# Two transformer blocks on one core: own buffers for the first four weight units, a new order of the element-wise steps in the feed-forwards, and an earlier turning of the second expert block's rows

## What is computed

```python
def reference(x, ...):
    x = first_block(x, ...)      # rms_norm, h @ w_in (5 x 512 + 288 + 2048 columns), fox attention, sparse attention, gates, w_out,
                                 # then x + hierarchical_moe(rms_norm(x)): 16 experts, 2 of them per token, SwiGLU, width 512
    return second_block(x, ...)

def second_block(x, ...):
    f = swiglu(rms_norm_2(h, ffn1_pre_g), ffn1_w_gu, ffn1_w_down)     # D_FF = 2816
    h = h + 0.5 * rms_norm_2(f, ffn1_post_g)
    ...                                                              # neighbourhood and latent attention, w_out
    f = swiglu(rms_norm_2(h, ffn2_pre_g), ffn2_w_gu, ffn2_w_down)
    h = h + 0.5 * rms_norm_2(f, ffn2_post_g)

def swiglu(h, w_gu, w_down):
    gate, up = jnp.split(h @ w_gu, 2, axis=-1)
    return (jax.nn.silu(gate) * up) @ w_down
```

## Time and profile before

| what | us |
|---|---|
| median of 3 runs (lowest, highest) | 1979.58 (1977.93, 1980.55) |
| the profiled execution, its own time | 1979.71 |
| span of the profiled execution | 1977.9 |
| PE busy in it | 1811.5 |
| DVE busy, ACT busy | 966.3, 858.6 |
| mean granted clock of TensorE | 0.947 |

### The profile page before, as it was taken

One profiled execution on the slowest core, in us unless ns is written; L12 is line 12 of the kernel. 1 busy time (PEld: TensorE's weight loads), 2 busy tenths in 40 slices (PEclk: granted clock), 3 DMA queues, 4 the chain that ended last, 5 costly groups with the idle time before them and its releaser, 6 DMA issues.

```text
span 1977.9 us, 22533 instructions
## 1 busy us (share of the span) xinstructions
PE 1811.5 (92%) x8483; PEld 1428.6 (72%) x8483; DVE 966.3 (49%) x1548; ACT 858.6 (43%) x1355; POOL 254.5 (13%) x313
## 2 busy tenths in 40 slices
PE   6997999999859999969999999898788989999997
PEld 5785566666748888857888888786564768888886
DVE  2536444435358999964332342634555353413434
ACT  4234555553237888853222222424566142213222
POOL 3100342320001111110000000331223000000000
PEclk8998899999969999988999999998789989999999
DMA  5323111113568999672323322233000123233331
GB/s 161 107 67 107 43 44 43 44 43 117 202 232 328 383 386 391 264 248 76 107 85 96 106 85 96 87 108 112 12 22 22 46 77 102 85 96 107 87 104 53
DMA packets 161283, 246.31 MB, mean 125 GB/s; under 512 B 11586, under 2 KB 117281, under 8 KB 148256
## 3 DMA queue, kind: packets, MB, share of 16 engines
q1 hardware_dynamic: 152880, 232.30, 34.8%
q0 software_dynamic: 8304, 12.69, 2.1%
HBM read 239.15 MB, written 12.61 MB: 127 GB/s over the span
## 4 chain that ended last, share of the span: by engine, by line
PE 83%; DVE 6%; ACT 4%; issue 3%; DMA 1%; POOL 1%; SPq 0%; DVEq 0%; ACTq 0%; POOLq 0%
PE psum L425 24%; PE psum L426 23%; PE psum L427 23%; PE psum L570 3%; PE psum L590 3%; PE psum L559 2%; ACT warea_r L410 2%; DVE warea_r L416 1%; PE psum L1232 1%; DMA warea<-in_w_in 1%; POOL arena L690 1%; PE psum L1138 1%; PE psum L1020 1%; DVE xarea L2214 1%; PE psum L1401 0%
## 5 line engine op out<-in xcount | busy, mean ns | idle before, releaser
L416 DVE TENSOR_TENSOR warea_r<-warea,warea_r 128x2048 fp32r<-128x2048 f32 x114 | 268.0, 2353 | 388.7 <-ACT warea_r L410 388.5
L425 PE MATMUL psum<-tarea_r,warea_r 128*128 128x512 f32 x896 | 358.2, 400 | 5.9 <-DVE arena_r L2235 3.9
L426 PE MATMUL psum<-tarea_r,warea_r 128*128 128x512 f32 x896 | 351.7, 393 | 0.0
L427 PE MATMUL psum<-tarea_r,warea_r 128*128 128x512 f32 x896 | 351.4, 392 | 0.0
L410 ACT ACTIVATE warea_r<-warea 128x2048 fp32r<-128x2048 f32 x114 | 217.2, 1907 | 303.2 <-PE psum L427 288.4
L425 PE MATMUL psum<-warea_r,arena_r 128*128 128x512 f32 (+1 forms) x768 | 300.8, 392 | 15.1 <-DVE arena_r L2180 7.3
L427 PE MATMUL psum<-warea_r,arena_r 128*128 128x512 f32 (+1 forms) x768 | 297.2, 387 | 0.0
L426 PE MATMUL psum<-warea_r,arena_r 128*128 128x512 f32 (+1 forms) x768 | 297.1, 387 | 0.0
L425 PEld LDWEIGHTS psum<-tarea_r,warea_r 128*128 128x128 f32 x896 | 169.5, 189 | 48.3 <-issue 7.7
L427 PEld LDWEIGHTS psum<-tarea_r,warea_r 128*128 128x128 f32 x896 | 169.9, 190 | 36.3
L426 PEld LDWEIGHTS psum<-tarea_r,warea_r 128*128 128x128 f32 x896 | 169.8, 190 | 34.1 <-issue 0.7
(11 more groups left out here) (321 smaller groups left out, 2436.2 us busy)
## 6 DMA issues: line engine op xcount, KB each, us to landing
warea<-in_ffn_w_gu SPq DMA_DIRECT2D x88, 512.0 KB, 4.9
warea<-in_w_in SPq DMA_DIRECT2D x48, 512.0 KB, 4.7
warea<-in_ffn_w_down SPq DMA_DIRECT2D x40, 512.0 KB, 4.4
arena<-in_w_up SPq DMA_DIRECT2D x16, 1024.0 KB, 7.3
tarea<-in_w_up SPq DMA_DIRECT2D x16, 1024.0 KB, 7.7
tarea<-in_w_down SPq DMA_DIRECT2D x16, 1024.0 KB, 8.0
warea<-in_w_gate SPq DMA_DIRECT2D x14, 1024.0 KB, 7.8
harea<-in_w_gate SPq DMA_DIRECT2D x14, 1024.0 KB, 8.1
```

The source lines that it names most:

```text
L416: dve.tensor_tensor(w_lo[:, u % 2, :], raw[:, u % RAW, :], w_hi[:, u % 2, :].bitcast(f32), ALU.subtract)\
L425: nc.tensor.matmul(out, high, by_high, start=first, stop=False)
L426: nc.tensor.matmul(out, high, by_low, start=False, stop=False)
L427: return nc.tensor.matmul(out, low, by_high, start=False, stop=last)
```

## The change

Five edits.

1. Units 0 to 3 are loaded into buffers of their own in the arena (`EARLY = 4`, `raw_of`, `unit_in`), with a semaphore each. Loads wait for a `split_low` only from unit 6 on. Unit 0 is issued after the second tile of `x`; unit 1 only when the fourth tile has landed, and all behind it. POOL issues the gain column first and holds its other small loads until the fourth tile and unit 0 have landed.
2. In a feed-forward chunk, ACT writes the high half of the hidden chunk ahead of `split_high(v + 2)`, and DVE the low half ahead of `split_low(v + 2)`.
3. `row_factor` of halves 0 and 2 stands right behind PE's chunk 0.
4. In expert round 0 PE turns the rows of block 1 ahead of the last of the four units of `gate_up(0)`; ACT's `slot_high(1)` waits for all of `gate_up(0)` (`moe_done` 8), since the halves have one buffer.
5. Semaphores: `mask_in` becomes `const_in` at 32; three of the bias table's loads on POOL become one and a chained memset; the wait between the two additions of the experts' results (L2214) is on DVE's own step counter in place of `y_used`.

```diff
+EARLY = 4
+    def raw_of(u):
+        return carve(2048 * u, 2048) if u < EARLY else raw[:, u % RAW, :]
+    def unit_in(u):
+        return (s[f"early{u}"], 32) if u < EARLY else (raw_in[u % RAW], 32 * ((u - EARLY) // RAW + 1))
...
-        act.wait_ge(raw_in[u % RAW], 32 * (u // RAW + 1) + (i * 16))
+        sem, value = unit_in(u)
+        act.wait_ge(sem, value + (i * 16))
...
             def feed(u):
-                if u >= RAW:
+                if u >= EARLY + RAW:
                     sp.wait_ge(s["split_lo"], u - RAW + 1)
...
                 sp.dma_start(xres[:, t, :], w["x"][0, t * P:(t + 1) * P, :]).then_inc(s[f"rows_in{t}"], 16)
-            for u in range(2):
-                feed(u)
+                if t == 1:
+                    feed(0)
+            sp.wait_ge(s["rows_in3"], 16)
+            feed(1)
...
             gain_column(0, "norm_mix_g", "col_in0")
+            pool.wait_ge(s["rows_in3"], 16)
+            pool.wait_ge(s["early0"], 32)
...
-            nc.gpsimd.memset(rpbs[0:120, :], 0.0).then_inc(s["rpb_zero"], 1)
-            pool.wait_ge(s["rpb_zero"], 1)
+            chained(nc.gpsimd.memset(rpbs[0:120, :], 0.0))
...
+                    if i == 2 and isinstance(b, int) and b == 0:
+                        slot_features(1)
...
                 gate_up(b)
-                slot_features(b + 1)
                 if not first:
+                    slot_features(b + 1)
                     down(b - 1, 4)
...
                     for k in range(2):
-                        if g % 2 == 0 and isinstance(v, int) and v == 1 and k:
-                            row_factor((2, 4)[g // 2], ps[7])
...
                     mm.then_inc(s["unit_done"], 1)
+                    if g % 2 == 0 and isinstance(v, int) and v == 0:
+                        row_factor((2, 4)[g // 2], ps[7])
...
             def slot_high(b):
+                if isinstance(b, int) and b == 1:
+                    act.wait_ge(s["moe_done"], 8)
...
                     nc.scalar.activation(sgb[:, v % 2, :], sgb[:, v % 2, :], ACT.Silu).then_inc(s["ff_silu"], 1)
-                    split_high(u0 + v + 2, i)
                     act.wait_ge(s["gated"], i + (base + v + 1))
                     at = hid_hi[:, v, :] if isinstance(i, int) else hid_hi[:, ds(i + v, 1), :].rearrange("p a q -> p (a q)")
                     nc.scalar.activation(at, sgb[:, v % 2, :], ACT.Copy).then_inc(s["hid_high"], 1)
+                    split_high(u0 + v + 2, i)
...
-                    split_low(u0 + v + 2, i)
                     dve.wait_ge(s["hid_high"], i + (base + v + 1))
...
                     V.tensor_tensor(lo, sgb[:, v % 2, :], hi.bitcast(f32), ALU.subtract).then_inc(s["ff_hid"], 1)
+                    split_low(u0 + v + 2, i)
...
-            dve.wait_ge(s["mask_in"], 16)
+            dve.wait_ge(s["const_in"], 32)
```

More of the change, by code:

```diff
@@ L340, in build_blocks @@
     Rp = nc.dram_tensor("rpb_padded", (H * 15, 64), f32, kind="Internal").ap()
-    names = """rows_in0 rows_in1 rows_in2 rows_in3 ident_in const_in mask_in col_in0 cols_late moe0 moe1 moe2 moe3 moe4 moe5 moe6 moe7 moe8 moe9 moe10 moe11
+    names = """rows_in0 rows_in1 rows_in2 rows_in3 early0 early1 early2 early3 ident_in const_in col_in0 cols_late moe0 moe1 moe2 moe3 moe4 moe5 moe6 moe7 moe8 moe9 moe10 moe11
         moe_hi moe_lo moe_done gain_in gain_used head_gain_in pos_in misc_in
@@ L402, in unit_through @@
         eng.wait_ge(s[sem], i + value)
+    def raw_of(u):
+        return carve(2048 * u, 2048) if u < EARLY else raw[:, u % RAW, :]
+    def unit_in(u):
+        return (s[f"early{u}"], 32) if u < EARLY else (raw_in[u % RAW], 32 * ((u - EARLY) // RAW + 1))
     def split_high(u, i=0):
         act = nc.scalar
-        act.wait_ge(raw_in[u % RAW], 32 * (u // RAW + 1) + (i * 16))
+        sem, value = unit_in(u)
+        act.wait_ge(sem, value + (i * 16))
         if u >= 2:
             unit_through(act, u - 2, i)
-        act.activation(w_hi[:, u % 2, :], raw[:, u % RAW, :], ACT.Copy).then_inc(s["split_hi"], 1)
+        act.activation(w_hi[:, u % 2, :], raw_of(u), ACT.Copy).then_inc(s["split_hi"], 1)
     def split_low(u, i=0):
@@ L415, in split_low @@
         dve.wait_ge(s["split_hi"], i + (u + 1))
-        dve.tensor_tensor(w_lo[:, u % 2, :], raw[:, u % RAW, :], w_hi[:, u % 2, :].bitcast(f32), ALU.subtract)\
+        dve.tensor_tensor(w_lo[:, u % 2, :], raw_of(u), w_hi[:, u % 2, :].bitcast(f32), ALU.subtract)\
             .then_inc(s["split_lo"], 1)
@@ L740, in feed @@
                     if width == 288 and cols == 8:
-                        dst = raw[:, u % RAW, 0:k * width].rearrange("p (c n) -> p c n", c=k)[:, :, at:at + cols]
+                        dst = raw_of(u)[:, 0:k * width].rearrange("p (c n) -> p c n", c=k)[:, :, at:at + cols]
                     else:
-                        dst = raw[:, u % RAW, at:at + k * width].rearrange("p (c n) -> p c n", c=k)[:, :, 0:cols]
-                    sp.dma_start(dst, src).then_inc(raw_in[u % RAW], 16)
+                        dst = raw_of(u)[:, at:at + k * width].rearrange("p (c n) -> p c n", c=k)[:, :, 0:cols]
+                    sp.dma_start(dst, src).then_inc(unit_in(u)[0], 16)
             masks = NCONST - CONSTS["na_mask"][1]
@@ L762, in _ @@
             sp.wait_ge(s["gate_scaled"], 16)
-            sp.dma_start(const[:, masks:NCONST], w["consts"][:, masks:NCONST]).then_inc(s["mask_in"], 16)
+            sp.dma_start(const[:, masks:NCONST], w["consts"][:, masks:NCONST]).then_inc(s["const_in"], 16)
             def expert_unit(b, i, e):
@@ L991, in _ @@
             pool.wait_ge(s["fd_psum"], 16)
-            nc.gpsimd.memset(rpbs[0:120, :], 0.0).then_inc(s["rpb_zero"], 1)
-            pool.wait_ge(s["rpb_zero"], 1)
[L994 to L997, removed]
+            chained(nc.gpsimd.memset(rpbs[0:120, :], 0.0))
+            pool.dma_start(rpbs[0:120, 16:47], w["na_rpb_2"][0].rearrange("h a b -> (h a) b")).then_inc(s["rpb_moved"], 16)
+            pool.wait_ge(s["rpb_moved"], 16)
+            pool.dma_start(Rp, rpbs[0:120, :]).then_inc(s["rpb_moved"], 16)
+            pool.wait_ge(s["rpb_moved"], 32)
             for h in range(H):
@@ L2211, in _ @@
                 for k in range(2):
[L2212 to L2216, removed]
+                    ins = V.scalar_tensor_tensor(out=xres[:, t, :], in0=Yt[t][:, D * k:D * k + D],
+                                                 scalar=wts[:, 4 * k + t:4 * k + t + 1], in1=xres[:, t, :],
+                                                 op0=ALU.mult, op1=ALU.add)
+                    if k == 0:
+                        chained(ins)
+                ins.then_inc(s["res_ready"], 1)
             raw_low(2)
```

6 lines of the change are left out of this document (3 added, 3 removed).

## The result

| | before | after |
|---|---|---|
| median, us (lowest, highest; runs) | 1978.76 (1975.79, 1980.55; 4) | 1958.47 (1957.22, 1959.91; 4) |
| span of the profiled execution | 1977.9 | 1957.7 |
| mean granted clock | 0.947 | 0.953 |

The ratio is 0.9899, with a 95% interval of 0.9882 to 0.9916: 20.3 us faster, where 16.8 were forecast. A later series of the same kernel gave 1959.78 against 1977.54, a ratio of 0.9908 [0.9895, 0.9921], or 17.8 us. The two intervals overlap. The estimates are 18 and 20 us, and the two intervals together reach from 16 to 23 us, so that more was won than the forecast's 16.8 is not shown.

The account below looks back on a forecast made before the run. PE's work, 83% of the chain that ended last, bounds the kernel, so only its waits and their clock losses can be won. -7.0 - 7.4 - 2.9 + 0.5 = -16.8 from 1979.6 gives 1962.8; range 1957 to 1968.5.

Parts of the forecast that it names:

- The beginning: First loads: x and unit 0 land at 12.6, PE's first product starts at 14.8 instead of 21.82, 7.0 us won.
- Clock at the beginning: PE's first products: still 5.6 us at 0.50 of its clock, so nothing counted, with 0 to 2.8 us to be had.
- Collision of POOL and DVE: After the beginning: POOL's squares start 0.03 us before DVE's split and block it 3.4 us; no gain counted.
- rival (a): Beginning gives more: DVE starts ahead of POOL, or full clock from the first product; 1958 to 1960, chance 0.14.
- Starts of halves 0 and 2: Feed-forward starts: row factor 5.4 us sooner, PE's 1.97 us wait and 1.7 us of clock go, twice; 7.4 us won.
- Ends of the halves: Last feed-forward chunk: PE's wait of 0.74 us for the low half goes in four halves, 2.9 us won.
- Experts: Between expert rounds: ACT now waits for round 0's last product, 0.5 us lost (0.3 to 0.7).
- Attention: Attention stage between the feed-forwards: the prediction gave no term for it.
- (b): First landing bound elsewhere: x and unit 0 complete at 16.8, or unit 1 late; 1967 to 1970, chance 0.16.
- (c): Beginning: POOL's load issues hold DVE's splits of units 0 and 1, at most 14 us; 1977, chance 0.04.
- (d): Steady feed-forward chunks: the later split makes PE wait, up to 1.4 us in each of 44; up to 2023, chance 0.04.

Follow-up runs that it names:

- that run: The changed kernel with DVE's split of unit 2 ahead of three small copies that wait for PE: 1953.77 against 1976.44, ratio 0.9885.

## Why the prediction was right

The time of 1958.47 lies in the range, 4.3 us under the forecast. By its steps:

- **The beginning, -7.0.** Right in mechanism and nearly in size. Forecast and found: last tile of x landed at 12.6 and 12.48, first product 14.8 and 15.18, unit 1's split on ACT no later than 20.5 (18.27 to 20.19). From the last tile's landing to the first product it took 2.7 us and not 2.2: PE had begun on the third tile only at 11.28, sixteen transposes at 0.23 us each kept it until 14.95, and the fourth tile stood behind the third. The landing came from the middle of two bounds, so its closeness is partly luck. The forecast blamed unit 1, the constants and POOL's loads alike; only the runs showed that POOL's loads were the disturbing part (3.5 us), that the held units and constants were no part of it (0.1 us), and that unit 0's place among the x tiles goes with the rest.
- **Clock at the beginning, 0 of 0 to 2.8.** Here the forecast was too low at first and right in the end. The first products ran slow for 1.5 us instead of 5.6, and the kernel was 9.6 us ahead at 48 us; the rest of that rise came behind unit 2's wait. Near 200 us it lost it again, from 10.2 us ahead to 7.4. The windows of the kernel before and of the changed one, over the same work:

```profile
200.00:220.00 20.00, 18.17 (x64) 9.46 (x63) 7.72 (x20) 10.48 (x23) 4.27 (x5) 0.71 0.34 105
```

```profile
190.00:210.00 20.00, 18.45 (x47) 9.33 (x48) 6.85 (x18) 8.31 (x17) 2.14 (x3) 0.56 0.34 106
```

  0.71 - 0.56 over 20 us is 3.0 us of full-clock work less. It does not come with the change each time: the second profiled execution of the changed kernel had 0.69 in its window from 190 to 210 and kept its lead of 9.2 us there, while the run with edit 1 alone lost 2.8. So such gains come and go. Why the clock stays low longer in one execution than in another stays open.
- **Collision of POOL and DVE.** It stayed, as the forecast had it, with 0.03 us between the two; the half of rival (a) that hung on it did not occur.
- **Starts of halves 0 and 2, -7.4.** 7.8 found. The row factor came at 900.42, 7.3 us in front of 907.7 because the kernel was 7.2 ahead, and the low half and the split followed as worked out. The 1.7 us of clock were real: PEclk stayed at 1.00, and the 3.9 us at each start are 2.13 of stall and 1.7 of clock. The run with edit 2 alone shows that the two edits are not a sum there.
- **Ends of the halves, -2.9.** This is the mis-sized term: 4.1 found, in four steps of 1.0 to 1.1 for waits of 0.74. The idle time in a row counts from the modelled end of the last matmul, 0.39 us behind its start, but in a running stream the next one starts 0.23 behind. A wait of 0.74 thus delays the next start by 0.90, and the first interval behind it was 0.33 (1027.59 to 1027.92) instead of 0.23: together 1.0. The same 0.16 is in each long stall: from 919.24 to 921.60 it is 2.36 from start to start, 2.13 more than 0.23, against the 1.97 of the row.
- **Experts, +0.5.** 0.48, by the same path as written: ACT's start moved to the last product.
- **Attention, 0.** 1.0 us came there (13.2 ahead to 14.2), and no edit has a part in it. The difference swings between 12.5 and 15.5 around 1380 us. Over the same work the granted clock was 0.73 in the kernel before (1360 to 1410) and 0.82 in the changed one (1347 to 1397), but 0.77 in the changed kernel's second execution (1346 to 1396), which lost 3.4 us against the first in this stage. The 1.0 us is within what two executions of one kernel differ by.
- **Rivals.** (b), a landing bound elsewhere, fell with 12.48. (c), POOL's issues hold DVE, fell: both splits took 2.29 us at 11.92 and 20.23 while POOL issued from 12.77 on. (d), the steady chunks wait, fell: the waits for a split are three with 7.4 us, as they were before (7.5). But the mechanism of (d) is not idle, since in the run with edit 2 alone it costs 2.67 us where the chunk starts late. (a), more from the beginning, was nearest: the time lies in its range of 1958 to 1960. The extra of its clock was spent by 215 us, and what the trace shows over the forecast, 20.1 against 16.8, is made up of the ends (1.2), the attention (1.0), the starts (0.4) and the beginning with the experts (0.7). Of these only the ends and the starts recur from trace to trace; the rest is of the size of the spread between two executions.

## What to carry to other kernels

When a wait is taken away by a new order in a queue, look at what is now last in that queue, and whether its first round starts late: edit 2 alone turned a wait of 1.97 us into one of 2.67, and with the late start cured it paid in full. Work that is moved earlier into a single buffer gains nothing until the buffer has a twin: 0.48 us lost with one, 2.7 won with two, both against the kernel before. A short stall of TensorE costs more than its row says, here 1.0 us for 0.74.

## What was not expected of the hardware

- **Small loads of another queue cost a large transfer more than large ones of its own.** POOL's loads in flight beside x and unit 0: first product 3.5 us later. A megabyte of unit 1 and the other constants issued right behind x on SP: 0.1 us.
- **The transposes run at the slow rate while the column says 1.00.** In the changed kernel the first thirty-two take 0.23 us each in windows with PEclk 1.00, those of the earlier trace rows 0.13 each, those of the earlier trace rows 0.25 each in a stretch at 0.50. So at the start of this program the column did not show the rate; the duration of a known instruction did. With earlier products on PE the transposes of the last two tiles took 0.14. Products are not needed for it: in the kernel before, where the third tile came 0.59 us after the second was through and not 2.32, the last two tiles took 1.41 and 1.10 us, 0.18 and 0.14 each, with only transposes ahead of them:

```profile
9.68 1.41 PE L1020 MATMUL psum<-const,xarea 128*128 128x128 f32 x8 [0.59 <-DMA xarea<-in_x]
```

  Unit 0's place between the tiles may thus have cost the last two tiles some of this speed; no run shows how much of that reached the first product.
- **A wait of 1.97 us was followed by a fall of the clock, the waits of 0.74 us were not**, and the fall cost nearly as much as the wait.
- **POOL held DVE while it read data, not while it issued loads.** A split took 3.92 us beside its squares and 2.29 beside its issues of loads, in that run and in the changed kernel.
